# Seam columns at group changes, wraps, prompt rows and octet parts reordered, row scaling a slot later, in the front stage of a hybrid encoder layer

## The reference, cut to what matters

```python
def encoder_layer(x, ...):                # x_prompt: 256 rows, x_sample: 2048 rows, 1024 wide
    xn = rms_norm(x, norm1)
    proj = xn @ w_in                      # 1024 -> 3*512 (hyena x0, x1, v) + 8*64 (q) + 2*64 (k) + 2*64 (v)
    uc = short_conv(proj[..., :1536], conv_w, conv_b)       # width 3, centred on the row
    x0, x1, v = split(uc)
    y_hy = x0 * bidir_long_conv(x1 * v, h_f, h_b, skip)     # rfft/irfft at twice the length
    y_at = window_gqa(q, k, v, ...)
    h = x + concat(rms_norm(y_hy), rms_norm(y_at)) @ w_out
    return h + swiglu(rms_norm(h) @ w_gate_up) @ w_down
```

## Time and profile before

| | |
|---|---|
| median of 3 runs | 2722.42 us (2719.92 to 2726.14) |
| the profiled execution | 2725.49 us |
| its span, first to last instruction | 2723.7 us |
| PE busy | 2614.8 us (96%) |
| DVE busy | 2105.7 us (77%) |
| ACT busy | 1371.5 us (50%) |
| POOL busy | 1233.3 us (45%) |
| mean granted TensorE clock | 0.987 |

### The profile page before, as it was taken

One profiled execution on the slowest core, in us unless ns is written; L12 is line 12 of the kernel. 1 busy time (PEld: TensorE's weight loads), 2 busy tenths in 40 slices (PEclk: granted clock), 3 DMA queues, 4 the chain that ended last, 5 costly groups with the idle time before them and its releaser, 6 DMA issues.

```text
span 2723.7 us, 39433 instructions
## 1 busy us (share of the span) xinstructions
PE 2614.8 (96%) x13881; PEld 2388.3 (88%) x13881; DVE 2105.7 (77%) x2508; ACT 1371.5 (50%) x2365; POOL 1233.3 (45%) x1182
## 2 busy tenths in 40 slices
PE   8899999899998999999999999999999989999998
PEld 6888889888896888878999999899999989999997
DVE  6765664688548777867888888988888898888887
ACT  5564544477437787764434434443434443443432
POOL 1655211112212444465677854455654444444443
PEclk9999999999998999999999999999999999999999
DMA  7687967899986464454444443543333354332332
GB/s 231 198 278 227 315 211 220 279 276 282 266 215 178 130 151 125 122 165 150 136 140 138 140 121 112 194 141 115 113 110 104 93 182 157 92 93 89 90 90 89
DMA packets 470044, 446.33 MB, mean 164 GB/s; under 512 B 54670, under 2 KB 377358, under 8 KB 469559
## 3 DMA queue, kind: packets, MB, share of 16 engines
q1 hardware_dynamic: 441960, 372.22, 47.1%
q0 software_dynamic: 27888, 71.58, 8.4%
HBM read 329.90 MB, written 113.79 MB: 163 GB/s over the span
## 4 chain that ended last, share of the span: by engine, by line
PE 83%; DVE 8%; DMA 3%; issue 2%; ACT 2%; SPq 2%; POOL 0%; DVEq 0%; ACTq 0%; POOLq 0%
PE ff_banks L85 17%; PE ff_banks L86 17%; PE ff_banks L87 17%; PE pr_acc L85 4%; PE pr_acc L86 4%; PE pr_acc L87 4%; PE am_mix L85 2%; PE am_mix L86 2%; PE am_mix L87 2%; DMA sp_k<-k_dram 2%; PE am_turn L2310 2%; PE pr_gen L85 1%; PE pr_gen L87 1%; PE pr_gen L86 1%; PE am_acc L2324 1%
## 5 line engine op out<-in xcount | busy, mean ns | idle before, releaser
L3445 DVE TENSOR_TENSOR ff_h<-ff_h,ff_banks 128x1536 f32<-128x1536 f32 x231 | 402.9, 1744 | 5.7 <-PE ff_banks L87 5.2
L3281 ACT COPY ff_r<-ff_banks 128x384 f32<-128x384 f32 x198 | 94.9, 479 | 590.2 <-PE ff_banks L87 590.1
L3428 DVE TENSOR_TENSOR ff_dlo<-ff_dlo_raw,ff_dhi 128x512 fp32r<-128x512 f32 x231 | 213.0, 922 | 172.7 <-ACT ff_dhi L3311 172.6
L85 PE MATMUL ff_banks<-ff_xhi,ff_ghi 128*128 128x384 f32 x924 | 313.5, 339 | 12.3 <-DVE ff_silu L3405 6.5
L85 PE MATMUL pr_acc<-pr_xhi,pr_whi 128*128 128x386 f32 (+1 forms) x864 | 304.7, 353 | 16.2 <-DVE pr_xlo L1639 16.2
L87 PE MATMUL ff_banks<-ff_xhi,ff_glo 128*128 128x384 f32 x924 | 311.6, 337 | 0.0
L85 PE MATMUL ff_banks<-ff_xhi,ff_uhi 128*128 128x384 f32 x924 | 310.8, 336 | 0.6 <-ACT ff_r L3281 0.6
L86 PE MATMUL ff_banks<-ff_xlo,ff_ghi 128*128 128x384 f32 x924 | 311.2, 337 | 0.0
L86 PE MATMUL ff_banks<-ff_xlo,ff_uhi 128*128 128x384 f32 x924 | 310.6, 336 | 0.0
L87 PE MATMUL ff_banks<-ff_xhi,ff_ulo 128*128 128x384 f32 x924 | 310.0, 335 | 0.0
L3129 POOL TENSOR_TENSOR ff_act<-ff_act,ff_silu 128x384 f32<-128x384 f32 x99 | 117.1, 1183 | 418.1 <-issue 235.5
(11 more groups left out here) (351 smaller groups left out, 6678.6 us busy)
## 6 DMA issues: line engine op xcount, KB each, us to landing
ff_glo_raw<-w_gate_up SPq DMA_DIRECT2D x132, 256.0 KB, 3.0
ff_ulo_raw<-w_gate_up SPq DMA_DIRECT2D x132, 256.0 KB, 2.9
ff_dlo_raw<-dsum_dram SPq DMA_DIRECT2D x132, 256.0 KB, 2.7
pr_raw<-w_in SPq DMA_DIRECT2D x108, 256.0 KB, 5.7
ff_dlo_raw<-w_down SPq DMA_DIRECT2D x99, 256.0 KB, 2.6
sp_k<-k_dram SPq DMA_DIRECT2D x64, 256.0 KB, 5.7
pr_xs<-x SPq DMA_DIRECT2D x18, 512.0 KB, 5.9
xkeep_dram<-pr_xs SPq DMA_DIRECT2D x18, 512.0 KB, 4.7
```

Source lines behind the costliest of these rows:

```text
L85: pe.matmul(out, still[0], moving[0], start=start, stop=False, skip_group_check=goes_on)
L3281: act.copy(kept[n][:], bank(X)).then_inc(copied, 1)
L3428: dve.tensor_tensor(dlo[d_slot(n)][:], din[d_slot(n)][:], dhi[d_slot(n)][:].bitcast(F32), ALU.subtract).then_inc(d_low, 1)
L3445: dve.tensor_tensor(to, to, lowered_all(k), ALU.add).then_inc(added, 1)
```

## The change

Six edits, all in `front`:

1. **Seam.** `turn(r, 2)` for r of 1 and more moves ahead of the last second half of the round before and leaves out its last column (384). Tile 3 is split: `lift(r, 3)` does its transpose and copy, and `turn(r, 3)`, now without the transpose, leaves out its first column (385). The new `seam(r)` copies and subtracts those two columns, 128x8 each, after the last chunk of the round before. Chunk 0 of the next round waits for tiles 0 to 2 and `seam` in place of tiles 0 to 3 (`rows_needed`, `edge_lows`). In rounds 2 and 5 two memsets move from `turn(r, 2)` to `turn(r, 3)` on DVE, and chunk 0's wait counts them still.
2. **Scaling a slot later.** `norm` is split into `squares` (ACT, place as before) and `scale` (DVE, later): tile 6r+5 behind `turn(r, 4)`, tile 6r+6 behind the eviction of unit 0's chunk 0, the four others behind the second half of chunk 1.
3. **Features ahead of wraps.** `wave_end(0, 1)` stands ahead of `wave_mid(1, 1)`.
4. **Prompt rows.** The two prompt tiles of u are loaded by one DMA in `first_u` to a place of their own, not by turns into the two buffers `us`.
5. **Octets.** The parts of octets 0 and 1 leave `product_step(0)` and `product_step(1)` and get two slots of their own, so that all later side work lies two slots later in the course.
6. SP waits one tile longer before it reloads the slot of tile 2 of a group.

```diff
-            turn(r, 2)
             if r:
+                lift(r, 3)
+                seam(r)
                 evict(r - 1, units_of(r - 1) - 1, 1)
                 yield
+            else:
+                turn(0, 2)
             turn(r, 3)
             if r == 0:
                 norm(GT - 2)
-            norm(GT * r + GT - 1)
+            squares(GT * r + GT - 1)
             if r:
                 yield
+            else:
+                scale(GT - 1)
...
                 if i == 0:
                     turn(r, 4)
+                    if r:
+                        scale(GT * r + GT - 1)
                     if r < ROUNDS - 1:
-                        norm(GT * r + GT)
+                        squares(GT * r + GT)
                 yield
                 if i == 0:
                     turn(r, 5)
                 second_half(r, i, 0)
                 evict(r, i, 0)
+                if i == 0 and r < ROUNDS - 1:
+                    scale(GT * r + GT)
                 if i == 0 and peeks(r):
                     turn(r, 6)
...
                 first_half(r, i, 1)
                 if 1 <= i <= 4 and r < ROUNDS - 1:
-                    norm(GT * r + GT + i)
+                    squares(GT * r + GT + i)
                 if i == end and r < ROUNDS - 1:
                     turn(r + 1, 1)
                 yield
+                if i == end and r < ROUNDS - 1:
+                    turn(r + 1, 2)
                 second_half(r, i, 1)
+                if 1 <= i <= 4 and r < ROUNDS - 1:
+                    scale(GT * r + GT + i)
...
+        wave_end(0, 1)
         wave_mid(1, 1)
-        wave_end(0, 1)
...
             return_step(j - 2)
             yield
+            if j == 1:
+                for t in range(2):
+                    octet_parts(t)
+                    yield
...
             bring_u(1)
+            sp.wait_ge(weighted, NTT)
+            sp.dma_start(prompt_u[:], u_rows[LS:T].rearrange("(t p) c -> p t c", p=P)).then_inc(skip_in, 16)
...
+        def seam(rd):
+            act.wait_ge(unit_done, 2 * first_unit(rd))
+            if rd < NG:
+                act.wait_ge(x_copied, 2 * (GT * rd + 3) + 2)
+            for s in range(2):
+                act.copy(xhi[:, :, SEAM + s:SEAM + s + 1], edge_rows(rd, s)).then_inc(edge_high, 1)
...
-            if not peeks(rd) and j == 2:
+            if not peeks(rd) and j == 3:
...
+        def seam(rd):
+            dve.wait_ge(edge_high, edge_highs(rd))
+            for s in range(2):
+                o = slice(SEAM + s, SEAM + s + 1)
+                dve.tensor_tensor(xlo[:, :, o], edge_rows(rd, s), xhi[:, :, o].bitcast(F32), ALU.subtract).then_inc(edge_low, 1)
```

More of the change, by code:

```diff
@@ L185, in peeks, with turned_span, edge_highs, edge_lows @@
         return r % NG < NG - 1
+    SEAM = 2 * P + P
+    def turned_span(r, j):
+        a, b = (0, P) if r == 0 or j not in (2, 3) else ((0, P - 1) if j == 2 else (1, P))
+        return slice(a, b), slice(place(r, j) + a, place(r, j) + b)
+    def edge_highs(r):
+        return sum((k != NG) + 2 for k in range(1, r + 1))
+    def edge_lows(r, seam=True):
+        return sum((0, 1, 3, 2, 1, 3)[k] + 2 for k in range(1, r + 1)) - 2 * (not seam)
     def turn_number(r, j):
@@ L231, in columns, with course, squares, scale @@
         return [(3 * HY + (HEADS + 2 * (i - 6)) * HD, P, 0)]
-    def course(now, norm_rows, weights, turn, u_turn, first_half, second_half, evict):
+    def course(now, norm_rows, scale_rows, weights, turn, lift, seam, u_turn, first_half, second_half, evict):
         UN = first_unit(ROUNDS)
-        def norm(n):
+        def squares(n):
             if n < NTT:
                 norm_rows(n)
+        def scale(n):
+            if n < NTT:
+                scale_rows(n)
+        def norm(n):
+            squares(n)
+            scale(n)
         norm(0)
@@ L366, in front @@
     vc = qe.sb("vc", [P, 2, CH])
+    prompt_u = Place(nc, "ur", pr.end + 40960).sb("us_prompt", [P, 2, HY])
     hs = Place(nc, "sp", pr.end)
@@ L1357, in turn @@
             n = GT * rd + j
[L1358 to L1363, removed]
+            if (rd >= NG or j < GT) and (rd == 0 or j != 3):
+                lift(rd, j)
             for h in range(2):
@@ L1373, in turn, with lift @@
                 else:
-                    act.copy(xhi[:, 4 * h:4 * h + 4, place(rd, j):place(rd, j) + P], got).then_inc(x_high, 1)
+                    t, o = turned_span(rd, j)
+                    act.copy(xhi[:, 4 * h:4 * h + 4, o], got[:, :, t]).then_inc(x_high, 1)
+        def lift(rd, j):
+            n, q = GT * rd + j, turn_number(rd, j)
+            if rd >= NG:
+                act.wait_ge(x_in[n % 5], 16 * (n // 5 + 1))
+                return
+            for h in range(2):
+                act.wait_ge(x_turned, 2 * q + h + 1)
+                act.copy(xs[:, n % 5, 512 * h:512 * h + 512], turned[:, h, :]).then_inc(x_copied, 1)
+        def seam(rd):
[4 more added lines that the diff above has]
+                act.copy(xhi[:, :, SEAM + s:SEAM + s + 1], edge_rows(rd, s)).then_inc(edge_high, 1)
         def u_turn(e):
@@ L1600, in scalar, with scale_rows @@
         now = [0]
-        woven(course(now, norm, weights, turn, u_turn, nothing, nothing, evict),
+        woven(course(now, norm, nothing, weights, turn, lift, seam, u_turn, nothing, nothing, evict),
               side(now, wave, nothing, wave_end, made_step, weigh_step, prompt, nothing, eighth,
-                   first_u, u_step, product_step, return_step, nothing, z_step, eighth_parts, z_parts, opening))
+                   first_u, u_step, product_step, return_step, nothing, z_step, eighth_parts, z_parts, octet_parts, opening))
     def vector(dve, opening):
-        def norm(n):
+        def scale_rows(n):
             if n == 0:
@@ L1862, in vector @@
         now = [0]
-        woven(course(now, norm, weights, turn, u_turn, nothing, nothing, evict),
+        woven(course(now, nothing, scale_rows, weights, turn, nothing, seam, u_turn, nothing, nothing, evict),
               side(now, wave, wave_mid, wave_end, made_step, weigh_step, nothing, nothing, eighth,
-                   first_u, u_step, product_step, return_step, first_z, z_step, eighth_parts, z_parts, opening))
+                   first_u, u_step, product_step, return_step, first_z, z_step, eighth_parts, z_parts, octet_parts, opening))
     def finished(engine):
```

55 lines of the change are left out of this document (36 added, 19 removed).

## The result

The changed kernel takes 2738.61 us (median of 4 runs, 2735.0 to 2741.44) where the kernel before takes 2722.08 (4 runs): a ratio of 1.0058, 95% interval 1.0044 to 1.0071, so 12 to 19 us slower. Its profiled execution took 2739.0 us with a span of 2737.2, 13.5 more than the span before, at a mean granted clock of 0.983 (before 0.987). PE, DVE, ACT and POOL are busy for 2622.9, 2111.9, 1373.7 and 1225.6 us. So PE is busy 8.1 us longer than before with the same 13881 matmuls, and idle 5.4 us longer: of the 13.5 us more in this pair of traces the larger part is matmuls at a lower clock, and the smaller part is waiting.

The account below looks back on a forecast made before the run. PE, busy for 96% of the span, was taken as the bound. Terms 4.3 + 4.9 + 3.0 + 1.0 + 0 - 4.5 - 0.5 + 0 gave +8.2 us, so 2730.6; range for 8 in 10: 2716 to 2738.

Parts of the forecast that it names:

- (c): Round 2: tile 5's transposes wait for the later row scaling; 3.0 us lost, 1.2 at full clock, 2.9 to 4.6 at low.
- (d): Features ahead of wraps: two waits become one of some 5 us for `fi_h`; 1.0 us lost, between 0 and 3.4.
- (g): Round 5: seam and memsets help chunk 0, PE waits 4 to 5 us for z; -0.5 us, bounds -2 and +2.
- (f): Prompt rows and octets, round 4: 8.6 us gained, about half left after the filter spectrum's load; -4.5, bounds -13 and -1.
- (a): Round 0, peek at tile 6: scaling behind the eviction delays PE's transposes to 39.6; 2.7 to 4.4 us lost, 4.3 taken.
- (b): Round 1: later scaling delays tile 5's transposes and the peek at tile 12; net 3.3 to 5.0 us lost, 4.9 taken.
- (e): Round 3, seam: chunk 0 starts earlier, but DVE is the bound and chunk 1 waits; 0 us, bounds -1.5 and +0.5.
- Losses and gains don't cancel: Denies the rival that no low-clock stretch is added and losses of 7.2 us meet gains of 5 to 8: 2721 to 2726; chance 0.28.
- the 6 that would have spoken against the forecast: Sign: prediction wrong if PE gains over 6 us between the last u step and the last return step.
- Faster: Rival: product steps bound by the DVE and ACT chain, not loads, and losses bare; -8.2 us, 2714; chance 0.12.
- Much slower: Rival: as forecast, but later z steps or spectrum loads stop PE repeatedly, two such waits giving 2742 us; chance 0.05.
- The seam does nothing: Rival: other waits (memsets, z) hold chunk 0; +2 us on the forecast, 2733; shares the forecast's chance of 0.55.

## Why the prediction was right or wrong, point by point

**The sum was half of what came.** The forecast was 8.2 us more, 2730.6; measured are 2738.61 and, by the ratio, 15.8 us more. That is 0.6 us above the upper end of the stated range, 2738. In the pair of traces it is 13.5 us, 5.3 more than forecast: (c) 1.8, (d) 0.65, (g) 1.6, the low clock in round 0 where no edit lies 1.7, the unchanged rest 2.3, less 2.2 of (f) and 0.5 of the others. The other 2 to 3 us lie in the profiled execution before, which took 3.4 us more than its kernel's median, while the one after took 0.4 more than its own.

**The direction and the main cause were right.** In (a) and (b) the scaling chains cost what the rows of ACT and DVE said. Here is (a) in the changed kernel, ACT and DVE between PE's second half and its transposes at 39.45:

```profile
36.03 0.67 ACT L1486 ACTIVATE pr_cx<-pr_acc,pr_cw 128x384 f32<-128x384 f32 x1
36.73 0.62 DVE L1752 SCALAR_TENSOR_TENSOR pr_cx<-pr_acc,pr_cw,pr_cx 128x384 f32<-128x384 f32 x1
37.39 0.62 DVE L1754 SCALAR_TENSOR_TENSOR pr_cx<-pr_acc,pr_cw,pr_cx 128x384 f32<-128x384 f32 x1
37.92 0.15 DVE L1687 RECIPROCAL pr_stat<-pr_stat 128x1 f32<-128x1 f32 x1
38.11 1.28 DVE L1689 SCALAR_TENSOR_TENSOR pr_xs<-pr_xs,pr_stat,pr_gbc 128x1024 f32<-128x1024 f32 x1
```

The forecast said 39.6 for the transposes and 2.7 to 4.4 for the price; the trace has 39.45, a wait of 2.47 and 4.1. **(b)** 4.9 forecast, 5.0 found, with both waits that it named: 2.01 ahead of tile 5's transposes and 3.46 at the peek.

**(c) was mis-sized**, 3.0 for 4.8, just over its upper bound of 4.6: the wait's chain was right, and its price in clock was too low. The chain is the one that was written down:

```profile
308.42 1.19 PE L1135 MATMUL pr_turned<-pr_ident,pr_xs 128*128 128x128 f32 x8
309.27 1.07 ACT L1437 COPY pr_xs<-pr_turned 128x512 f32<-128x512 f32 x2 [1.59 <-PE pr_turned L1135]
310.23 1.15 ACT L1428 CAST pr_xhi<-pr_xs 128x512 fp32r<-128x512 f32 x2
310.89 1.30 DVE L1716 TENSOR_TENSOR pr_xlo<-pr_xs,pr_xhi 128x512 fp32r<-128x512 f32 x2 [2.32 <-ACT pr_xhi L1428]
312.11 0.16 DVE L1687 RECIPROCAL pr_stat<-pr_stat 128x1 f32<-128x1 f32 x1
312.30 1.28 DVE L1689 SCALAR_TENSOR_TENSOR pr_xs<-pr_xs,pr_stat,pr_gbc 128x1024 f32<-128x1024 f32 x1
```

From 308.42 to 313.64 are 5.2 us, 5.0 forecast. I had taken the middle of "full clock, 1.2" and "low clock, up to 4.6". There was no reason for a middle: a gap of over 3.5 was forecast (4.02 came), and all gaps of 3.5 and more in my own rows had a stretch behind them. My list of short gaps without a stretch also left out the gap of 1.50 at 292.75, which had two (0.57 over 292 to 300) and 2.07 us of idle time of PE just ahead of it.

**(d)** 1.0 forecast, 1.65 found at its place. The wait was called rightly, one of about 5 for `fi_h` (4.42), and its price is one stretch of low clock more than before, inside the bounds of 0 and 3.4. The 1.7 us ahead of it aren't the edit's: they follow this wait for POOL, which the edit doesn't touch,

```profile
69.68 0.77 PE L1165 MATMUL pr_turned<-pr_ident,pr_cx 128*128 128x128 f32 x3 [1.39 <-POOL pr_cx L942]
```

and two kernels without the edit lose as much there: the one with the scaling alone 1.7 us, the one with seam, prompt rows and octets 1.6. The price at the place scatters. From the last half of unit 3 to that of unit 5 in round 0 the six traces with this edit lose 1.6 to 3.4 us on the kernel before; those with the old order lie between 1.8 gained and 1.8 lost. At the end the edit on its own costs nothing that can be measured.

**(e)** 0 forecast, -0.35 found: DVE is the bound there, and the wait moved from chunk 0 to chunk 1.

**(f) was near in size, and its second half was told wrongly.** By the course the two edits won 9.3 us up to the second half of round 4, unit 1 (16.8 behind before and 7.55 there), 8.6 forecast. But at that place 18 side matmuls (3.2 us) are still owed to the two empty slots. Then half was to be lost to the first spectrum load. The wait of 3 us for DVE's product did come (3.39 at 588.84), but it isn't a loss against before, whose longest such wait was 3.6. Between that second half and unit 9, before and after:

```profile
543.32:677.65 134.33, 122.42 (x656) 112.23 (x654) 111.32 (x137) 98.69 (x162) 27.09 (x53) 0.99 1.04 282
```

```profile
550.87:687.78 136.91, 126.30 (x668) 115.52 (x667) 112.01 (x138) 101.59 (x166) 25.45 (x50) 0.98 1.06 288
```

After, PE is busy for 126.30 us in place of 122.42, with 12 matmuls more, and idle for 136.91 - 126.30 = 10.6 in place of 11.9. So the 2.6 us that come back in this stretch are not more waiting. Of the 3.9 us more of busy time, 2.2 are the 12 side matmuls that the two empty slots had put off, and 1.7 is one stretch more of low clock (0.98 for 0.99 above). What I had counted as the load's share was work put off, most of it, and never won. The loads bind both kernels about alike; who DVE's products waited for in the changed kernel and in the one before (us, times):

```profile
  DMA sp_k<-k_dram: 16.1, 6
```

```profile
  DMA sp_k<-k_dram: 17.2, 8
```

**(g)** -0.5 forecast, +1.1 found, inside its bounds. The seam gives 5.6 at chunk 1 of unit 0, and the z wait of 4.5 us with its low clock takes 6.0 back; the wait was forecast at 4 to 5. One thing was missed: with the side two slots later, the last return step falls into the change of round, and DVE's low part of y stands behind the subtractions of round 5's first tiles:

```profile
697.73 1.07 ACT L1631 CAST sp_yhi<-sp_yf 128x1024 fp32r<-128x1024 f32 x1
698.03 2.50 DVE L1716 TENSOR_TENSOR pr_xlo<-pr_xs,pr_xhi 128x512 fp32r<-128x512 f32 x4
...
700.44 1.22 DVE L1889 TENSOR_TENSOR sp_ylo<-sp_yf,sp_yhi 128x1024 fp32r<-128x1024 f32 x1
```

The cast was done at 698.8, the subtraction began at 700.44, and PE waited 2.49 us for it. I had weighed what the two slots give, not what the steps that slide with them meet on DVE.

**The rest of the kernel** was put at 0 and shows +2.3, in code that doesn't differ. The same part ran between 4.5 us shorter and 3.7 us longer than before in the traces of the experiments, whose code there doesn't differ either. So 2.3 us in one trace can't be put down to an edit. The same holds inside the front stage: the kernel with the octets back is the changed kernel up to round 4, and yet at round 1, unit 0, chunk 1 its trace is 15.1 us behind where the other is 12.4. Single terms below 2 us in the table above are therefore no more than signs.

**The rivals.** Losses and gains don't cancel: the scaling alone (19 us) is four to five times what prompt rows and octets win. PE gained 2.4 us from the end of the last u step (526.94 before, 539.45 after) to unit 9 of round 4, well under the 6 that would have spoken against the forecast. "Faster" needed small losses and product steps free of the loads, and had neither. "Much slower" has its time, 2742 beside 2738.6, but not its mechanism. "The seam does nothing" fits what can be measured, and for another reason: in round 3 it wins chunk 0 and loses it at chunk 1.

The rule of the Trainium skill on small operations ("VectorE: DVE Perf Modes", TRN2 errata) changes nothing visible here: the seam's ten subtractions on DVE (128x8, out of SBUF) took 0.17 us each, PE waited for none of them, and the seam cost no measurable time.

## What to carry to other kernels

Before a step of a feeding engine is moved later, look for its consumer on the bound engine and for what already stands in front of it on the feeding engine: of the six scalings of a group four were free to move, and the other two, which PE's transposes asked for at once, cost some 17 us over three rounds: 12 of waiting, the rest most likely clock. When a wait is removed, find what else the same later work hangs on; in round 3, in the kernel with scaling and wraps as before, the seam gained 3.5 us at chunk 0 and lost 4 at chunk 1. To hide a load's latency, add the cover behind its issue, not ahead of it, and check what every step that slides along will meet on the other queues.

## What the runs showed of the hardware that I had not expected

Shorter gaps than I had rows for can come with a low granted clock: the one of 2.47 us at 39.45 had 1.7 us missing around it (0.79 over 36 to 44), and even the one of 1.39 us at 69.68 (0.79 over 68 to 76); a z wait of 1.20 us had none (1.00 over 696 to 704), and neither had the gap of 2.01 us at 172.62 (1.00 over 169 to 177). So the length of a gap alone doesn't tell whether a stretch comes. And the clock isn't the same from one execution to the next. The kernel with the octets back has the same code up to round 4, and about the same wait at the same place (1.99 us ahead of 173.01; 2.01 ahead of 172.62), but a clock of 0.79 where the changed kernel was granted 1.00. First the changed kernel, then the other:

```profile
169.00:177.00 8.00, 4.84 (x28) 3.90 (x26) 4.91 (x8) 6.84 (x14) 1.46 (x3) 1.00 1.02 367
```

```profile
169.00:177.00 8.00, 6.01 (x26) 5.30 (x25) 4.43 (x7) 6.66 (x13) 1.86 (x3) 0.79 1.06 382
```
